# Moving the arena of a fused two-block kernel by 192 bytes: base addresses at multiples of 128 bytes

## The chip, the core and the metric

The kernel runs on one core of a Trainium2 chip. Its engines are TensorE (matmuls, weight loads), VectorE, ScalarE and GpSimd; SyncE issues most of the DMA transfers. They share SBUF, a memory of 128 partitions, and meet through semaphores. The metric is the device time of one execution in microseconds; lower is better.

## The reference

Two transformer-like blocks run one after the other on 256 tokens of 1024 features, all in float32. Cut to what matters here:

```python
def reference(x, ...):
    h = concat(meta_tokens, x)                 # 16 + 256 tokens
    h = h + token_mixer(h)                     # retention + mLSTM heads, w_in, w_out
    h = h + expert_choice_ffn(h)               # 16 experts, 34 tokens each, D_FF = 2816
    x = rmsnorm(h)[:, 16:]
    for layer in range(2):                     # second block
        x = x + rmsnorm(mixer[layer](rmsnorm(x)))           # attention / conv, then RG-LRU
        x = x + rmsnorm(memory_cross_attention(rmsnorm(x), rmsnorm(mem)))
        x = x + rmsnorm(swiglu(rmsnorm(x)))                 # D_FF = 2816
    return x

def expert_choice_ffn(h):
    ...                                        # per expert: its 34 top tokens
    hid = silu(xs @ w_gate[e]) * (xs @ w_up[e])
    y = hid @ w_down[e] * g[e]
```

The experts' weights (16 times three matrices of 1024 x 2816) are by far most of what has to be read from memory.

## The kernel before

The program is written out by hand, one instruction stream for each engine, with semaphores between them; nothing is scheduled by a tool. It has three parts, one after the other.

- Part A, the mixer of the first block, to about 200 us. Weights come in chunks of 1 MB into a ring. ScalarE writes a rounded copy of each chunk ("high") and VectorE the remainder ("low"), and TensorE makes three passes (high x high, low x high, high x low), lines 865, 883 and 1082. The moving operands are mixer_high_a, mixer_high_b and mixer_low, eight tiles of 272 columns (1088 bytes) each.
- Part B, the 16 experts, to about 1500 us. For each expert SyncE loads w_gate, w_up and w_down in quarters of 2816 KB into the ring, each as soon as TensorE has read the quarter that it replaces (line 587). `hidden` (line 1266) has the token tile xs as weights and streams the ring; the down projection (line 1349) has hidT as weights and streams the ring. In between, eight pieces of w_xkv for the second block are loaded into the arena (line 593, tile kvw) and used at line 1233.
- Part C, the second block, to the end. Chunks of 1 MB come into the ring again and are split in high (ScalarE, line 2174) and low (VectorE, line 2915). `in_part` (through `three_passes`, line 1394) has the weights chunk as stationary operand and streams input_high or input_low, 256 columns. `token_part` (line 1425) does the reverse: the stationary operand is input_high or input_low, and the ring is streamed. The output projections (`out_half`, also through line 1394) stream 512 columns of the ring.

All tiles lie in a few large SBUF tensors that are allocated one behind the other: weight_ring (W), ident, ones, hT (the residual stream), squares (SQ), rstd, vec_cols (VC), gate_w, router_w, small and arena (Z). `z(cols, at)` gives a slice of the arena, and `rounded` puts a tensor of the rounded type over a place of an existing one:

```python
def sb(name, cols, dt=F32):
    made = ctx.enter_context(nc.sbuf_tensor(name, [P, cols], dt))
    BASE[name] = nc.sbuf_base - 4 * cols
    return made
...
def rounded(name, over, at, cols):
    offset = BASE[over] + 4 * at
    return nc.alloc_sbuf_tensor_at(name, [P, cols], F32R, offset=offset)[:]
...
kvw = z(2 * 2 * D, 8192)
xs = z(KT * MPAD, 21280)
th = z(P * HF, 21808)
hidT = z(P * HF, 23216)
...
x_high = rounded("input_high", "arena", 14336, 2 * D)
x_low = rounded("input_low", "arena", 16384, 2 * D)
y_high = rounded("mixed_high", "weight_ring", CSLOTS * CSLOT, 2 * D)
```

The numbers are columns of 4 bytes. So a tile's address in a partition is the base of its tensor and four times its column. mixed_low (column 18432) and hidden_high_a (20480) lie in the arena too, mixed_high in the ring, and hidden_low_b in hT. A column number that is a multiple of 32 is an offset that is a multiple of 128 bytes.

Of the kernel before, what the change touches and what calls it, by code (L numbers as in the profile page):

```python
# [31 lines left out]
DFF = 2816  # L32
FT = DFF // P
EPS = 1e-6
ARENA = 25096
BIG = 1e30
PAD = 2

# [89 lines left out]
def build(nc, t, out):  # L128

    with ExitStack() as ctx:  # L130
        BASE = {}
# [5 lines that stand above are left out]
# [3 lines left out]
        def S(name):  # L140
            if name not in sems:
                sems[name] = ctx.enter_context(nc.semaphore(name))
            return sems[name]
# [7 lines left out]
        hT = sb("hT", KT * T)  # L151
        SQ = sb("squares", KT * T)
        RSTD = sb("rstd", T)
        VC = sb("vec_cols", 256)
        GW = sb("gate_w", KT * 16)
        RW = sb("router_w", KT * 16)
        small = sb("small", 192)
        Z = sb("arena", ARENA)

        def rounded(name, over, at, cols):  # L160
# [4 lines left out]
        def vec(name, i):  # L165
            tile, at, n = VEC_AT[name]
            return VC[:, tile * P + at + i:tile * P + at + i + 1]

        def vec_cols(name, n):
            tile, at, _ = VEC_AT[name]  # L170
            return VC[:, tile * P + at:tile * P + at + n]

        cursor = [0]

        def z(cols, at=None):
            if at is None:
                at = cursor[0]
                cursor[0] += cols
            assert at + cols <= ARENA, (at, cols)
            return Z[:, at:at + cols]  # L180
# [18 lines left out]
        lamt = small[:, 144:152]  # L199
        n4sp = small[:, 152:160]  # L200
        stat = small[:, 160:176]
        eps = small[:, 184:185]
        tiny = small[:, 185:186]


        uT = z(KT * T)
# [15 lines left out]
        rows = [z(T) for _ in range(7)]  # L222
        assert cursor[0] <= ARENA, cursor[0]
        vrow = QKP[:, 0:256]
# [41 lines left out]
        mm = z(2 * KT * 256, 12288)  # L266
        mem_gains = VC[:, 192:208]
        utok = z(TT * D, 16384)
# [2184 lines left out]
        def _(dve):  # L2453
# [41 lines left out]
            for j, n in enumerate(VEC_COUNT):  # L2495
                last = dve.tensor_copy(VC[:, P * j:P * j + n], bank[7][:, T + P * j:T + P * j + n])
            last.then_inc(S("small_ready"), 1)
# [17 lines left out]
            dve.memset(qkp[:, :, PAD + T:2 * PAD + T], 0.0).then_inc(S("small_ready"), 1)  # L2515
            dve.tensor_scalar(half_a, VC[:, B_A_AT:B_A_AT + 8], 0.5, None, ALU.mult)
            dve.tensor_scalar(half_i, VC[:, B_A_AT + 8:B_A_AT + 16], 0.5, None, ALU.mult).then_inc(S("small_ready"), 1)
            lam = VC[:, LAM_AT:LAM_AT + 8]
# [823 lines left out]
```

## Time and profile before

| | |
|---|---|
| Median of 3 runs | 2224.81 us (2224.5 to 2226.95) |
| Profiled execution, span | 2224.9 us (the page gives no other time of it) |
| TensorE busy (matmul) | 2099.5 us, 94% |
| TensorE busy (weight load) | 1310.1 us, 59% |
| VectorE busy | 780.3 us, 35% |
| ScalarE busy | 627.7 us, 28% |
| GpSimd busy | 44.6 us, 2% |
| Moved by DMA | 725.27 MB, mean 326 GB/s |

Busy times overlap, so they don't add up to the span. An engine's share of the span is an average over three parts with different limits; the chain of work that ended last tells which engine set the end in which part. Matmuls are pipelined, and the time from the start of one to the start of the next is shorter than the duration that the profile gives for one.

### The profile page before, as it was taken

The numbers are of one execution on the slowest core, as the hardware profiler recorded it, in microseconds if no ns is written. First come the engines' busy times: TensorE is split into PE (matmuls) and PEld (weight loads), VectorE is DVE, ScalarE is ACT, GpSimd is POOL, SyncE is SP. The second block draws the span as 40 slices with busy tenths as digits, with TensorE's granted clock in tenths as the row PEclk, the third lists the DMA queues.
The fourth block names the chain that finished last, engine by engine and source line by source line (L and its number), as shares of the span: only waits on it lengthen the run. The fifth ranks groups of instructions, "written<-read, shape, count | busy, mean of one in ns | idle before, by whom it ended". The sixth has DMA issues, their size and how long they took to land.

```text
span 2224.9 us, 27202 instructions
## 1 busy us (share of the span) xinstructions
PE 2099.5 (94%) x12031; PEld 1310.1 (59%) x12031; DVE 780.3 (35%) x1144; ACT 627.7 (28%) x988; POOL 44.6 (2%) x74
## 2 busy tenths in 40 slices
PE   9999999898898999989899899889999999999999
PEld 9987443333333443434333333327889998998997
DVE  8984211011010111111011011016666565876553
ACT  6564100000000000000000000005565444965442
POOL 3201000000000000000000000000000000000000
PEclk9999999999999999999999999999999999999999
DMA  7548999999999999999999999997454656554653
GB/s 235 167 136 352 417 431 428 431 428 431 428 430 430 427 429 429 428 430 429 429 430 430 429 430 430 429 425 241 146 171 155 202 184 197 174 170 151 198 189 114
DMA packets 146527, 725.27 MB, mean 326 GB/s; under 512 B 8678, under 2 KB 106522, under 8 KB 119658
## 3 DMA queue, kind: packets, MB, share of 16 engines
q1 hardware_dynamic: 145224, 721.53, 81.1%
q8 instruction: 95, 1.56, 0.3%
q0 software_dynamic: 640, 1.37, 0.2%
q10 hardware_dynamic: 546, 0.63, 0.1%
q14 instruction: 22, 0.18, 0.0%
HBM read 722.44 MB, written 1.07 MB: 325 GB/s over the span
## 4 chain that ended last, share of the span: by engine, by line
PE 65%; DMA 27%; DVE 5%; ACT 1%; issue 1%; SPq 1%; DVEq 0%; ACTq 0%
PE bank L1394 24%; PE bank L1266 18%; DMA weight_ring<-in_w_gate_dram 10%; DMA weight_ring<-in_w_up_dram 9%; DMA weight_ring<-in_w_down_dram 8%; PE bank L1349 6%; PE bank L1233 5%; PE bank L1425 3%; DVE weights_ring L2480 1%; PE bank L1197 1%; PE bank L1082 1%; DVE arena L2540 1%; PE bank L1324 1%; PE bank L1611 1%; PE bank L1741 1%
## 5 line engine op out<-in xcount | busy, mean ns | idle before, releaser
L1266 PE MATMUL bank<-weight_ring,arena 128*64 128x506 f32 x3024 | 634.6, 565 | 65.4 <-DMA weight_ring<-in_w_up_dram 42.6
L1266 PEld LDWEIGHTS bank<-weight_ring,arena 128*64 128x64 f32 x3024 | 219.8, 135 | 464.6 <-issue 374.6
L1349 PE MATMUL bank<-weight_ring,arena 128*64 128x512 f32 x1408 | 323.2, 610 | 40.1 <-DMA weight_ring<-in_w_down_dram 40.0
L2915 DVE TENSOR_TENSOR weights_ring<-weight_ring,weights_ring 128x2048 fp32r<-128x2048 f32 x110 | 249.7, 2289 | 126.3 <-ACT weights_ring L2174 125.9
L1394 PE MATMUL bank<-input_high,weights_ring 128*128 128x256 f32 x1920 | 248.3, 281 | 0.9 <-issue 0.9
L1349 PEld LDWEIGHTS bank<-weight_ring,arena 128*64 128x64 f32 x1408 | 99.2, 140 | 244.3 <-issue 185.5
L1394 PEld LDWEIGHTS bank<-input_high,weights_ring 128*128 128x128 f32 x1920 | 234.6, 188 | 2.9 <-issue 2.6
L2174 ACT ACTIVATE weights_ring<-weight_ring 128x2048 fp32r<-128x2048 f32 x109 | 205.8, 1908 | 60.2 <-DMA weight_ring<-in_w_ffn_down_dram 41.1
L2872 DVE TENSOR_TENSOR arena<-arena,bank 128x512 f32<-128x512 f32 x48 | 33.0, 688 | 498.9 <-PE bank L1233 498.9
L2070 ACT ACTIVATE arena<-bank 128x506 f32<-128x506 f32 (+1 forms) x48 | 23.5, 563 | 398.3 <-PE bank L1266 398.3
L1394 PE MATMUL bank<-input_low,weights_ring 128*128 128x256 f32 x960 | 132.3, 279 | 0.0
L1233 PE MATMUL bank<-arena 128*128 128x256 f32 x512 | 127.6, 392 | 0.0
L1233 PEld LDWEIGHTS bank<-arena 128*128 128x128 f32 x512 | 92.0, 189 | 52.7 <-issue 42.8
L1394 PEld LDWEIGHTS bank<-input_low,weights_ring 128*128 128x128 f32 x960 | 121.3, 188 | 0.0
L2090 ACT ACTIVATE squares<-bank 128x512 f32<-128x512 f32 x16 | 9.6, 597 | 382.7 <-PE bank L1349 382.7
L2040 ACT ACTIVATE squares<-bank 128x512 f32<-128x512 f32 x15 | 9.0, 597 | 367.5 <-PE bank L1197 367.5
L2861 DVE TENSOR_TENSOR hT<-hT,bank 128x512 f32<-128x512 f32 x60 | 38.6, 684 | 201.6 <-PE bank L1285 201.6
L1394 PE MATMUL bank<-weights_ring,mixed_high 128*128 128x512 f32 x320 | 93.7, 399 | 0.0
L2881 DVE SCALAR_TENSOR_TENSOR arena<-arena,bank 128x506 f32<-128x506 f32 (+1 forms) x48 | 28.0, 639 | 136.8 <-ACT arena L2070 136.8
L1394 PE MATMUL bank<-weights_ring,hidden_high_a 128*128 128x512 f32 x256 | 70.4, 395 | 0.0
L2870 DVE COPY arena<-bank 128x512 f32<-128x512 f32 x16 | 11.1, 692 | 167.5 <-PE bank L1233 167.5
L1394 PEld LDWEIGHTS bank<-weights_ring,mixed_high 128*128 128x128 f32 x320 | 59.5, 188 | 13.3 <-issue 0.2
(431 smaller groups left out, 2080.0 us busy)
## 6 DMA issues: line engine op xcount, KB each, us to landing
weight_ring<-in_w_down_dram SPq DMA_DIRECT2D x62, 2816.0 KB, 21.8
weight_ring<-in_w_up_dram SPq DMA_DIRECT2D x61, 2816.0 KB, 19.5
weight_ring<-in_w_gate_dram SPq DMA_DIRECT2D x60, 2816.0 KB, 18.9
weight_ring<-in_w_ffn_gu_dram SPq DMA_DIRECT2D x44, 1024.0 KB, 5.1
weight_ring<-in_w_ffn_down_dram SPq DMA_DIRECT2D x22, 1024.0 KB, 4.9
weight_ring<-in_w_in_dram SPq DMA_DIRECT2D x16, 1024.0 KB, 5.9
arena<-in_w_xkv_dram SPq DMA_DIRECT2D x8, 2048.0 KB, 21.2
weight_ring<-in_ab_w_in_dram SPq DMA_DIRECT2D x12, 1024.0 KB, 7.7
```

The costliest lines, as they stand in the source:

```text
L1082: last = pe.matmul(bank[pj.entries[A_OUT[n]][0]][:, 0:T], (high, low, high)[part][:, i, c], mix_low[:, T * i:T * i + T] if part == 2 else ...
L1233: last = pe.matmul(bank[7][:, 256 * a:256 * a + 256], w, x, start=(i == 0), stop=(i == 1))
L1266: last = pe.matmul(bank[first_bank + c][MPAD * half:MPAD * half + MPAD, 0:(hi - lo) * HF], xs3[:, s, :], w[:, lo:hi, HF * half:HF * half + ...
L1349: last = pe.matmul(bank[6][MPAD * half:MPAD * half + MPAD, :], hidT[:, at:at + MPAD], W[:, j * D + 512 * half:j * D + 512 * half + 512], s ...
L1394: last = pe.matmul(dst, w, y, start=start and n == 0, stop=stop and n == len(todo) - 1, skip_group_check=check)
L1425: last = pe.matmul(dst[:, 256 * t:256 * t + 256], x[:, i, tok], w[:, i, :], start=(n == 0 and i == 0), stop=(n == 2 and i == KT - 1))
L2070: act.activation(th[:, HF * lo:HF * hi], bank[c][:, 0:HF * (hi - lo)], ACT.Tanh, scale=0.5)\
L2174: act.activation(high_slot(k), raw_slot(k), ACT.Copy).then_inc(S("weights_high"), 1)
L2861: dve.tensor_tensor(rows, rows, bank[6 + n % 2][:], ALU.add).then_inc(S("scatter_taken"), 1)
L2872: ins = dve.tensor_tensor(dst, dst, bank[7][:], ALU.add)
L2881: dve.scalar_tensor_tensor(out=v, in0=v, scalar=1.0, in1=bank[c][:, 0:HF * (hi - lo)], op0=ALU.add, op1=ALU.mult)\
L2915: dve.tensor_tensor(low_slot(k), raw_slot(k), high_slot(k), ALU.subtract).then_inc(S("weights_low"), 1)
```

## The change

Four tensors of small tables lose unused columns and a spacer of 8 columns (32 bytes) is put ahead of the arena. vec_cols goes from 256 to 208 columns, small from 192 to 184 with its last two columns in use moved to 176 and 177, and the arena loses 8 unused columns at its end. Nothing else is edited: every instruction is the same, on the same engine, with the same waits and in the same order.

```diff
-ARENA = 25096
+ARENA = 25088
...
         hT = sb("hT", KT * T)
         SQ = sb("squares", KT * T)
         RSTD = sb("rstd", T)
-        VC = sb("vec_cols", 256)
+        VC = sb("vec_cols", 208)
         GW = sb("gate_w", KT * 16)
         RW = sb("router_w", KT * 16)
-        small = sb("small", 192)
+        small = sb("small", 184)
+        sb("arena_offset", 8)
         Z = sb("arena", ARENA)
...
-        eps = small[:, 184:185]
-        tiny = small[:, 185:186]
+        eps = small[:, 176:177]
+        tiny = small[:, 177:178]
```

Where the tensors begin in a partition, from the memory maps of the two built programs:

| Tensor | before, byte | past a multiple of 128 | after, byte | past a multiple of 128 |
|---|---|---|---|---|
| weight_ring | 16512 | 0 | 16512 | 0 |
| hT | 107648 | 0 | 107648 | 0 |
| squares | 116352 | 0 | 116352 | 0 |
| vec_cols | 126144 | 64 | 126144 | 64 |
| gate_w | 127168 | 64 | 126976 | 0 |
| router_w | 127680 | 64 | 127488 | 0 |
| small | 128192 | 64 | 128000 | 0 |
| arena | 128960 | 64 | 128768 | 0 |

## Rows read from the trace of the kernel before

**Rows 1.** The page: DMA rate in 40 slices; chain that ended last.

```profile
DMA  7548999999999999999999999997454656554653
GB/s 235 167 136 352 417 431 428 431 428 431 428 430 430 427 429 429 428 430 429 429 430 430 429 430 430 429 425 241 146 171 155 202 184 197 174 170 151 198 189 114
...
PE 65%; DMA 27%; DVE 5%; ACT 1%; issue 1%; SPq 1%; DVEq 0%; ACTq 0%
```

**Rows 2.** DMA: queue (packets, MB) and issues (count, KB each, us to landing).

```profile
q1 hardware_dynamic: 145224, 721.53, 81.1%
...
arena<-in_w_xkv_dram SPq DMA_DIRECT2D x8, 2048.0 KB, 21.2
...
arena<-in_w_up_dram SPq DMA_DIRECT2D x4, 1408.0 KB, 8.5
```

**Rows 3.** Line 593's loads of w_xkv; then two stretches, DMA share and GB/s last.

```profile
L593 SPq DMA_DIRECT2D arena<-in_w_xkv_dram x8: 328/432/434, 245.9 to 1214.9; - x8
...
DMA to landing us min/median/max: 12.4/21.2/24.0
...
250.00:1250.00 1000.00, 922.19 (x4404) 372.38 (x4401) 126.88 (x235) 89.60 (x148) 0.00 (x0) 0.98 1.00 429
1250.00:1450.00 200.00, 178.80 (x846) 68.52 (x846) 19.56 (x36) 16.60 (x26) 0.00 (x0) 0.98 1.01 430
```

**Rows 4.** Line 1394: duration ns min/median/max, first and last start us.

```profile
L1394 PE MATMUL bank<-input_high,weights_ring x1920: 276/279/468, 1537.5 to 2156.9; 128*128 128x256 f32 x192
L1394 PE MATMUL bank<-input_low,weights_ring x960: 276/279/283, 1539.4 to 2157.8; 128*128 128x256 f32 x192
L1394 PEld LDWEIGHTS bank<-weights_ring,mixed_high x320: 186/188/192, 1605.1 to 2179.3; 128*128 128x128 f32 x160
L1394 PEld LDWEIGHTS bank<-weights_ring,hidden_high_a x256: 187/188/189, 1820.9 to 2202.1; 128*128 128x128 f32 x128
```

**Rows 5.** The chain, in part C: start us, us, what.

```profile
1530.94 4.88 PE bank L1425 x43
1644.26 2.73 PE bank L1394 x24
1703.91 3.18 PE bank L1425 x27
1711.04 170.15 PE bank L1394 x1193
1759.92 6.13 PE bank L1394 x52
```

**Rows 6.** Line 1394 in two stretches: PE and PEld busy, granted clock, DMA.

```profile
1644.00:1648.00 4.00, 2.97 (x24) 2.79 (x24) 1.00 1.02 400
1760.00:1764.00 4.00, 4.00 (x37) 4.00 (x35) 1.00 0.84 263
```

**Rows 7.** Weight loads of the experts: duration ns min/median/max.

```profile
L1266 PEld LDWEIGHTS bank<-weight_ring,arena x3024: 132/134/229, 205.8 to 1485.8; 128*64 128x64 f32 x189
L1349 PEld LDWEIGHTS bank<-weight_ring,arena x1408: 132/137/232, 251.1 to 1509.7; 128*64 128x64 f32 x176
```

**Rows 8.** The page's groups: busy us, mean ns, idle before us.

```profile
L1266 PEld LDWEIGHTS bank<-weight_ring,arena 128*64 128x64 f32 x3024 | 219.8, 135 | 464.6 <-issue 374.6
L1349 PEld LDWEIGHTS bank<-weight_ring,arena 128*64 128x64 f32 x1408 | 99.2, 140 | 244.3 <-issue 185.5
```

**Rows 9.** VectorE lines 3217, 2861 and 2872: duration ns min/median/max.

```profile
L3217 DVE TENSOR_TENSOR mixed_high<-squares,hidden_high_a x8: 684/685/687, 1718.0 to 2086.6; 128x512 fp32r<-128x512 f32 x8
L3217 DVE TENSOR_TENSOR mixed_low<-squares,hidden_high_a x8: 684/685/686, 1761.0 to 2131.9; 128x512 fp32r<-128x512 f32 x8
L3217 DVE TENSOR_TENSOR hidden_low_b<-squares,hidden_high_b x6: 684/685/687, 1806.3 to 2165.8; 128x512 fp32r<-128x512 f32 x6
L2861 DVE TENSOR_TENSOR hT<-hT,bank x60: 680/684/689, 301.0 to 1479.3; 128x512 f32<-128x512 f32 x60
L2872 DVE TENSOR_TENSOR arena<-arena,bank x48: 687/689/689, 437.4 to 1377.9; 128x512 f32<-128x512 f32 x48
```

**Rows 10.** ScalarE lines 2296 and 2144: duration ns min/median/max.

```profile
L2296 ACT ACTIVATE mixed_high<-bank x8: 597/598/600, 1658.6 to 2016.7; 128x512 fp32r<-128x512 f32 x8
L2144 ACT ACTIVATE input_high<-bank x24: 593/597/601, 1519.4 to 2038.0; 128x512 fp32r<-128x512 f32 x24
```

**Rows 11.** The chain, in part A: start us, us, what.

```profile
107.08 3.01 PE bank L883 x24
171.91 12.31 PE bank L1082 x94
```

## The prediction, made before the changed kernel was timed

> **What bounds the kernel now.** I read the page first. Its slices show two regimes: from about 200 us to 1450 us the DMA engines are full at 417 to 431 GB/s, and outside that stretch they are not, while TensorE is busy nearly throughout [rows 1]. The chain of work that ended last says the same in shares: TensorE 65% of the span, DMA 27%, VectorE 5%, ScalarE 1% [rows 1]. So a change of addresses has four ways to act: it can change how fast DMA packets are written, how fast TensorE streams or loads operands, and how long a VectorE or a ScalarE instruction takes. It adds, removes and reorders nothing: instructions, waits and queue order of the two built programs are equal on all five engines.
>
> **What moves, and what does not.** From the memory map of the two programs: weight_ring starts at byte 16512, hT (the stream) at 107648, squares at 116352, before and after alike. All three are multiples of 128 already (129, 841 and 909 times 128) and do not move. gate_w, router_w, small and the arena move down by 192 bytes. The arena goes from 128960 (64 past a multiple of 128, 192 past one of 256) to 128768 (a multiple of both). A tile in the arena is helped only if its own offset is a multiple of 128: input_high, input_low, mixed_low, hidden_high_a, the expert input xs and the loads of w_xkv go from 64 past to aligned. The expert tiles th (offset 87232, 681.5 times 128) and hidT (92864, 725.5 times 128) go the other way, from aligned to 64 past. So half of the claim is no change at all, and the trace of before already holds the same instructions on tiles of both kinds. I price each engine from such pairs.
>
> **DMA.** Queue q1 moves 721.53 MB [rows 2]. All weight slots are in the ring and keep their addresses. Into the arena go the 8 loads of w_xkv (2048 KB each) and 4 of w_up (1408 KB) as the large ones [rows 2]. The first is issued at 245.9 us and the last at 1214.9 us, landing 12 to 24 us later [rows 3]. The stretch 250 to 1250 us, which holds nearly all of that traffic, moves 429 GB/s; the stretch 1250 to 1450 us, which has only ring loads, 430 GB/s [rows 3]. If the whole difference of 1 GB/s were the fault of unaligned writes, and all of it lay on the path, its removal would give 1000 us times 1/430, which is 2.3 us. I take 0, because 1 GB/s is the last digit of the view; the bounds are -2.3 us and 0, since no large load becomes less aligned.
>
> Here a rule speaks for the change. The Trainium skill, DMA: Bandwidth & Descriptors, section How a descriptor splits into AXI transactions, says that a descriptor which does not start at a multiple of 256 bytes first transfers from the 256-byte boundary below, and that the unused bytes cost beats of 32 bytes. For a row of w_xkv (16 KB at 192 past the boundary) that would be 6 beats on top of 512; by that rule, and as an estimate, 16 MB in such rows would take 1.2% longer than need be, some 0.5 us of the 39 us that 16.8 MB take at 430 GB/s; the sum would then be -0.5 us instead of 0. The trace neither confirms nor excludes so little, and the ring, which starts 128 past a multiple of 256, would keep its own cost under this rule.
>
> **TensorE, moving operand.** This is the term that could matter, for in the last third TensorE is the chain with few breaks: one piece from 1711 us on holds 1193 matmuls of line 1394 in 170.15 us [rows 5]. The projections (in_part, line 1394) stream input_high and input_low, 256 columns, from the unaligned arena: 1920 + 960 matmuls [rows 4]. The token parts (line 1425) stream 256 columns from the aligned ring. In the chain, 24 of the first kind take 2.73 us, 113.8 ns each, and 43 of the second take 4.88 us, 113.5 ns each [rows 5]. Elsewhere both are slower by the same: 52 of the first in 6.13 us are 117.9 ns each, and 27 of the second in 3.18 us are 117.8 ns [rows 5]. So there are two paces of streaming, at a granted clock of 1.00, the full 2.4 GHz level, in both cases [rows 6], and each pace is reached by aligned and unaligned operands alike. Alignment to 128 is worth at most 0.3 ns per matmul: 2880 times 0.3 ns is 0.9 us. I take 0, with bounds of 0.9 us either way.
>
> **TensorE, weight loads.** LDWEIGHTS of 128 columns has a median of 188 ns from mixed_high (aligned, in the ring) and 188 ns from hidden_high_a (unaligned, in the arena) [rows 4]. In the experts xs (unaligned) has a median of 134 ns and hidT (aligned) 137 ns [rows 7]. These two swap kinds; if 3 ns were due to that, xs would lose or gain 3024 times 3 ns, 9.1 us, and hidT 1408 times 3 ns, 4.2 us, with opposite signs, 4.9 us net. It is hidden: the weight-load side of TensorE sits idle 464.6 us before line 1266 and 244.3 us before line 1349 [rows 8]. Only if that cover were gone would 4.9 us show, so the term is 0.
>
> **VectorE and ScalarE.** The same subtraction of 512 columns (line 3217) into mixed_high (aligned), mixed_low (unaligned) and hidden_low_b (aligned) has medians of 685, 685 and 685 ns [rows 9]. An addition onto hT (aligned, line 2861) takes a median of 684 ns, one onto the arena (line 2872) 689 ns [rows 9]. ScalarE's copy from PSUM takes 598 ns into mixed_high and 597 ns into input_high [rows 10]. The widest gap is 5 ns in 684, 0.7%. VectorE holds 5% of the chain, 111 us, so even if every one of these instructions changed by that much it would be 0.8 us; ScalarE's 1% gives less than 0.1 us. I take 0, with bounds of 0.8 us either way.
>
> **Sum.** 0 us, with bounds of -2.3 - 0.9 - 0.8 = -4.0 us and +0.9 + 0.8 = +1.7 us. The page gives the profiled execution a span of 2224.9 us and no other time; the median of the three runs is 2224.81 us, 0.1 us below it, so the sum carries over as it stands: 2224.8 us. The runs themselves spread from 2224.5 to 2226.95 us, and I call 0.2%, 4.4 us, what a measurement of this kernel can tell from no change.
>
> **Rivals.** (1) Faster: the slower pace of 117.9 ns is a clash between operands that lie half a 128-byte line apart, and goes when ring and arena lie in step. Then 2880 matmuls fall by 4.1 ns, 11.8 us: 2213 us. It becomes visible from 1.5 ns each. For it: most of the projections run at the slower pace. Against it: the row of 24 at 113.8 ns is the same line on the same unaligned tile [rows 5], so address alone does not set the pace. Chance 0.09.
>
> (2) Slower: ring and arena in step make TensorE's two reads (weights from the ring, moving operand from the arena) meet. The nearest row for an uneven pace is line 1082, whose operands of 272 columns begin at alternating multiples of 64: 94 take 12.31 us, 131.0 ns each, against 24 in 3.01 us, 125.4 ns, at line 883 [rows 11]. That is 4.5%; on 117.9 ns it is 5.3 ns, times 2880 is 15 us: 2240 us. It too decides from 1.5 ns each. Against it: the token parts have no pace of their own, and line 883 has the same alternation as line 1082. Chance 0.05.
>
> (3) The change does nothing that the chip sees, for 64 past a line is as good as the line itself. This is the forecast: 2224.8 us, chance 0.86, its own range 2221 to 2229 us.
>
> **How the numbers follow.** Faster by over 0.2%: rival 1, 0.09. Slower: rival 2, 0.05. Within 0.2%: 0.86. For the range I take the bounds of the sum, 2220.8 and 2226.5 us, and add the spread of the runs at the upper end (2.1 us): 2228.6. Rounded outwards a little it is 2220.3 to 2229.2 us, and leaves out about the two rivals.
>
> **What the profile after would show.** Right: 429 GB/s in the stretch 250 to 1250 us, 188 ns for the weight loads, 685 ns for line 3217, the chain's projections again at 113.8 and 117.9 ns, and the same shares. Wrong would be a new pace of line 1394 (below 116 or above 119.5 ns in the long stretch from 1711 us), 431 GB/s or more where w_xkv is loaded, or an L1349 weight load above 140 ns, which would mean that hidT pays for its new place. The prediction fails if a relation between two operands' addresses counts, since the rows of before show each kind of tile but only one distance between ring and arena.

## The result, and the profile after

The changed kernel took 2228.78 us (median of 20 runs, 2227.77 to 2230.22), the kernel before in the same session 2225.32 us: a ratio of 1.0016 with an interval of 1.001 to 1.0022. That is 3.5 us more. It lies inside the predicted range (2220.3 to 2229.2 us) and inside 0.2%, but the interval does not hold 1: the change made the kernel a little slower, where the forecast was no effect at all. One execution of the kernel before took 4057.97 us and is left out.

First the page of the changed kernel, against [rows 1, 2, 8]; its span is 2227.1 us.

```profile
PE 65%; DMA 27%; DVE 5%; ACT 1%; issue 1%; SPq 0%; DVEq 0%; ACTq 0%
...
L1350 PEld LDWEIGHTS bank<-weight_ring,arena 128*64 128x64 f32 x1408 | 102.0, 143 | 252.1 <-issue 194.1
...
arena<-in_w_xkv_dram SPq DMA_DIRECT2D x8, 2048.0 KB, 21.5
```

The shares of the chain are those of before, within a point. Line numbers are one higher (line 1394 is now 1395, line 1425 is 1426). Now the stretches, as in [rows 3]: us, then busy PE, PEld, DVE, ACT and POOL, granted clock, DMA share and GB/s.

```profile
250.00:1250.00 1000.00, 928.74 (x4392) 371.80 (x4388) 125.33 (x231) 88.64 (x145) 0.00 (x0) 0.98 1.00 429
1250.00:1450.00 200.00, 180.88 (x854) 69.32 (x856) 19.55 (x36) 16.59 (x26) 0.00 (x0) 0.98 1.00 430
1712.00:1874.00 162.00, 162.00 (x1149) 151.89 (x1148) 86.25 (x62) 69.95 (x55) 0.00 (x0) 1.00 0.57 189
```

DMA runs as before, 429 and 430 GB/s. So does the clock: it is granted in full, 1.00, in part C.

The chain in part C shows the difference: start us, us, what. A piece of the chain is a stream of matmuls with nothing between them, so its time over its count is the pace from one start to the next.

```profile
1527.93 5.98 PE bank L1426 x48
1643.08 2.85 PE bank L1395 x24
1693.66 5.70 PE bank L1426 x48
1710.30 171.11 PE bank L1395 x1193
2049.24 172.53 PE bank L1395 x1199
```

And the same pieces before, apart from those in [rows 5]:

```profile
1530.07 5.76 PE bank L1425 x48
1660.76 2.83 PE bank L1394 x24
1694.47 5.44 PE bank L1425 x48
2047.95 171.56 PE bank L1394 x1199
```

The reader is to see two things. First, the pace. Leaving aside the pieces of 2.9 us and more, which both kernels have, 24 matmuls of the projections take one time after the change, 2.85 us (2.84 to 2.88), which is 2.85 / 24 = 118.8 ns each. Before there were two, 2.83 / 24 = 117.9 ns and 2.73 / 24 = 113.8 ns [rows 5]. Second, the length of part C. The first piece of part C and the end of its last give the sum: before 2047.95 + 171.56 - 1530.07 = 689.44 us, after 2049.24 + 172.53 - 1527.93 = 693.84 us, 4.4 us more. Summed over this chain, the 3732 matmuls of line 1394 take 538.14 us before and 542.09 us after, 3.95 us more, and the 480 of line 1425 take 58.07 and 58.83 us, 0.76 us more; the rest takes 0.3 us less. The two longest pieces alone carry 1.9 us (0.96 + 0.97). Part C began 2.1 us earlier in this execution than in the one before. The kernels below, profiled once each, reach the same piece between 1527.13 and 1528.84 us, whatever their addresses, so I don't put those 2.1 us down to the change.

### The profile page after: what moved, and what is told of

Its sections match the earlier page's. It is cut to its first block, busy times and chain, and to the rows that moved or that the text cites. A ratio compares the mean times of both kernels' runs of the same rounds, so it can differ in the third digit from the quotient of the medians.

```text
span 2227.1 us, 27202 instructions
## 1 busy us (share of the span) xinstructions
PE 2110.9 (95%) x12031; PEld 1314.9 (59%) x12031; DVE 779.8 (35%) x1144; ACT 627.1 (28%) x988; POOL 44.1 (2%) x74
## 4 chain that ended last, share of the span: by engine, by line
PE 65%; DMA 27%; DVE 5%; ACT 1%; issue 1%; SPq 0%; DVEq 0%; ACTq 0%
PE bank L1395 24%; PE bank L1267 17%; DMA weight_ring<-in_w_up_dram 12%; DMA weight_ring<-in_w_down_dram 9%; PE bank L1350 7%; DMA weight_ring<-in_w_gate_dram 6%; PE bank L1234 5%; PE bank L1426 3%; DVE weights_ring L2481 1%; PE bank L1198 1%; DVE arena L2541 1%; PE bank L1083 1%; PE bank L1325 1%; PE bank L1612 1%; PE bank L1635 1%
## 5 line engine op out<-in xcount | busy, mean ns | idle before, releaser
L1350 PE MATMUL bank<-weight_ring,arena 128*64 128x512 f32 x1408 | 333.6, 626 | 40.2 <-DMA weight_ring<-in_w_down_dram 40.2
L1350 PEld LDWEIGHTS bank<-weight_ring,arena 128*64 128x64 f32 x1408 | 102.0, 143 | 252.1 <-issue 194.1
## 6 DMA issues: line engine op xcount, KB each, us to landing
arena<-in_w_xkv_dram SPq DMA_DIRECT2D x8, 2048.0 KB, 21.5
```

Of the source, the lines that this page charges most:

```text
L1350: last = pe.matmul(bank[6][MPAD * half:MPAD * half + MPAD, :], hidT[:, at:at + MPAD], W[:, j * D + 512 * half:j * D + 512 * half + 512], s ...
```

## The experiments

Two theories stood against each other at first. Theory 1: what counts is how far TensorE's moving tile lies from its stationary tile (arena against ring), whatever the alignment of either. As it was first recorded it took this distance modulo 128: slow at a multiple of 128, as before halfway between. The rival: alignment itself counts (the arena at a multiple of 128), or the moved tables do. "Distance" below means the address of the arena tile less that of the ring tile, modulo 256, since the runs came to need 256 and not 128. It is (128960 - 16512) mod 256 = 64 before and 128 after; the tiles' own columns add multiples of 256.

**Tables alone.** vec_cols and small are trimmed as in the change (gate_w and router_w lose nothing, they only move), and a wider spacer puts the arena back at 128960: distance 64.

```diff
-        sb("arena_offset", 8)
+        sb("arena_offset", 56)
```

> The small tables are trimmed and moved as in the change, the arena stays at byte 128960 as before. After the change the second block (from the first matmul of line 1234/1350 that no longer waits for an expert's weights, about 1475 us, to the end) is 4.3 us longer than before, and the projections of 256 columns follow each other at 118.8 ns instead of 117.9. Theory 1 (the distance between ring and arena, now a multiple of 128, disturbs TensorE's two reads): 1.0000 of before, pace 117.9. Theory 2 (the arena's own alignment does it): the same here, 1.0000. Theory 3 (the tables' places, or chance): 1.0016, pace 118.8.

**Arena at 128896**, a multiple of 128 as in the change, but at distance 0.

```diff
-        sb("arena_offset", 8)
+        sb("arena_offset", 40)
```

> As the change, but the arena 128 bytes further up, at 128896: a multiple of 128 still, and now in step with the ring modulo 256 too. Theory 1 (distance to the ring is a multiple of 128): slow, 1.0016, pace 118.8 ns. Theory 2 (arena aligned to 128): slow, 1.0016. A variant of either with 256 in place of 128 would make this one differ: further from before (over 1.002) if ring and arena in step modulo 256 is what hurts, 1.0000 if the arena at a multiple of 256 is.

**Ring up by 64.** The arena stays at 128768 as in the change, the ring goes to 16576: arena aligned, distance 64 again.

```diff
+        sb("ring_offset", 16)
...
-        small = sb("small", 184)
-        sb("arena_offset", 8)
+        small = sb("small", 176)
```

> Ring, ident, ones, stream, squares and tables 64 bytes further up, the arena at 128768 as in the change: arena aligned, ring 64 past a multiple of 128, the distance 64 past one as before. Theory 1 (distance): 1.0000, pace 117.9. Theory 2 (the arena's own alignment): 1.0016, pace 118.8.

**Both 64 past a multiple of 128.** The ring at 16576 and the arena at 128832: nothing aligned, distance 128.

```diff
+        sb("ring_offset", 16)
...
-        small = sb("small", 184)
-        sb("arena_offset", 8)
+        small = sb("small", 176)
+        sb("arena_offset", 16)
```

> Ring 64 bytes up and the arena 64 bytes up too: both 64 past a multiple of 128, the distance a multiple of 128. Theory 1 (distance): slow, 1.0016, pace 118.8. Theory 2 (the arena's own alignment): 1.0000, pace 117.9.

In the last two, the two columns in use at the end of small move to 60 and 61. The four were measured against the same runs of the kernel before (2224.24 us, 2216.28 to 2227.07):

| Kernel | Arena | Distance | Median us (lowest to highest) | Ratio to before |
|---|---|---|---|---|
| tables alone | 64 past | 64 | 2224.87 (2219.8 to 2226.77) | 1.0005 (0.9995 to 1.0015) |
| arena at 128896 | aligned | 0 | 2228.35 (2227.19 to 2230.25) | 1.0025 (1.0015 to 1.0035) |
| ring up by 64 | aligned | 64 | 2224.29 (2219.89 to 2226.37) | 1.0 (0.999 to 1.0011) |
| both 64 past | 64 past | 128 | 2229.81 (2229.49 to 2230.18) | 1.0032 (1.0021 to 1.0043) |

The split goes by the distance and not by alignment: two kernels at distance 64, one with its arena aligned and one not, run as before; the two at 0 and at 128, one with ring and arena aligned and one with neither, are slower. The tables have no effect that these runs can tell (1.0005, at most 1.0015), and part C with them is as long as before, 689.56 us against 689.44. The chain of each shows the pace, first tables alone:

```profile
1658.13 2.73 PE bank L1395 x24
1651.40 2.83 PE bank L1395 x24
1708.30 170.16 PE bank L1395 x1193
```

Arena at 128896:

```profile
1660.81 2.87 PE bank L1395 x24
1711.01 170.70 PE bank L1395 x1193
```

Ring up by 64:

```profile
1659.90 2.73 PE bank L1395 x24
1710.07 165.97 PE bank L1395 x1193
```

Both 64 past:

```profile
1660.78 2.85 PE bank L1396 x24
1711.20 171.12 PE bank L1396 x1193
```

At 64 there are 2.73 and 2.83 us, at 128 2.85, at 0 2.87. The piece of 1193 at distance 0 is shorter than at 128 although its projections are slower (2.87 / 24 = 119.6 ns); the sweep below explains a part of that. And the piece of 1193 took 170.16 us in one kernel at distance 64 and 165.97 us in another: the same stream, both at the same distance, 4.2 us apart. Theory 1 had no word for two paces at one distance.

**Distance 192.** The changed kernel with the tiles of part C moved up by 64 bytes in the arena. (mixed_high in the ring, hidden_low_b in hT and hidden_high_b at the arena's start stay.)

```diff
-        x_high = rounded("input_high", "arena", 14336, 2 * D)
-        x_low = rounded("input_low", "arena", 16384, 2 * D)
-        y_low = rounded("mixed_low", "arena", 18432, 2 * D)
+        x_high = rounded("input_high", "arena", 14352, 2 * D)
+        x_low = rounded("input_low", "arena", 16400, 2 * D)
+        y_low = rounded("mixed_low", "arena", 18448, 2 * D)
...
-        WORK = 20480
+        WORK = 20496
```

> The changed kernel with its aligned arena, but the operand tiles of the second block (input_high, input_low, mixed_low and everything from WORK on) 16 columns, 64 bytes, further up inside it. Theory 1 (what counts is the distance of each of these tiles from the weights in the ring, modulo 128): the loss goes, 1.0000 of before, pace 117.9 ns or the lower 113.3. Rival (the loss sits in the arena's base, that is in the experts or the first mixer too): 1.0016 as after the change.

**The same edit on the kernel before**, whose distance goes from 64 to 128 by it.

> The kernel before, with the same operand tiles of the second block 64 bytes further up, nothing else moved: they come to lie a multiple of 128 from the ring (a multiple of 128, odd, as after the change). Theory 1: slow, 1.0016 to 1.003, pace 118.8 ns to 120 and no stretch at 113.3. Rival (the arena's base as a whole): 1.0000.

Both stand against the same runs of the kernel before (2225.21 us). The changed kernel with the shift took 2213.8 us (2213.47 to 2215.79), a ratio of 0.995 (0.9937 to 0.9964); the kernel before with the same shift 2229.7 us (2228.6 to 2231.36), 1.0022 (1.0013 to 1.0031). One edit of four numbers has opposite signs on two bases, and the second is the slowdown of the change brought about with every tensor at its old base. The first is a miss for Theory 1 as recorded: modulo 128 the distances 64 and 192 are one, and it expected 1.0000. Distance 192:

```profile
1527.39 5.94 PE bank L1426 x48
1658.10 2.73 PE bank L1395 x24
1708.14 165.45 PE bank L1395 x1193
2040.05 166.87 PE bank L1395 x1199
```

Before with the shift, distance 128:

```profile
1660.58 2.85 PE bank L1394 x24
1711.11 171.08 PE bank L1394 x1193
```

At 192 the long pieces are 5.7 us shorter each than after the change, and part C as a whole takes 2040.05 + 166.87 - 1527.39 = 679.53 us, 9.9 us less than before and 14.3 us less than after.

**Distances by themselves.** A kernel of matmuls alone; the reference's computation is left out. For each distance it streams 96 matmuls in the form of the projections (line 112 has distance 0, and each second line 16 bytes more, to line 142), then some in the form of the token parts (lines 144 to 150: 0, 64, 128, 192) and 48 of 512 columns (lines 152 to 158: the same four). The whole is done once with the other engines still and once with them at work (lines 162 to 208).

```diff
+            for n in range(16): pe.matmul(bank[6][:, 0:P], ident[:], ident[:], start=True, stop=True)
+            for n in range(96): pe.matmul(*in_args(n, 64), **ends(n, 24))
```

> Not the reference's computation: it leaves out all of it and only streams matmuls, 96 for each distance between the tile of the weights and the moving tile (0 to 240 bytes in steps of 16 modulo 256), as the projections do, then the two reverse forms at 0, 64, 128 and 192; all once with the other engines quiet and once with VectorE, ScalarE and DMA at work. Theory 1: at distances 0 and 128 the matmuls of 256 columns follow each other at 118.8 to 120 ns, at 64 and 192 at 113.3 or 117.9; with the engines quiet as well, since only TensorE's own two reads meet. Rival (the other engines' accesses to SBUF are what meets TensorE's): 113.3 at every distance while they are quiet.

Its chain, the whole of a line in each row:

```profile
28.32 11.51 PE bank L112 x96
...
88.08 11.31 PE bank L120 x96
...
117.89 11.52 PE bank L124 x96
...
132.98 10.93 PE bank L126 x96
...
147.48 11.40 PE bank L128 x96
...
207.27 11.31 PE bank L136 x96
...
326.72 10.92 PE bank L152 x48
...
341.22 11.19 PE bank L154 x48
...
355.98 11.15 PE bank L156 x48
...
370.70 10.99 PE bank L158 x48
...
492.84 10.93 PE bank L176 x96
```

Divided by 96: distance 0 is 119.9 ns, 64 is 117.8, 96 is 120.0, 112 is 113.9, 128 is 118.8, 192 is 117.8. All sixteen lie between 113.9 and 120.0 ns. With 512 columns the order is another one: 227.5 ns at 0, 233.1 at 64, 232.3 at 128, 229.0 at 192. So at distance 0 the 256-column matmuls lose and the 512-column ones gain. The piece of 1193 is a mix: 935 of 256 columns, and 258 of 512, of which 204 have their stationary tile in the arena. From 128 to 0 the first lose 1.0 us by these paces and the 204 gain 1.0. By that it should be about as long at 0 as at 128; that it was 0.4 us shorter stays unexplained. The second pass repeats the first (10.93 us again at 112), with VectorE and ScalarE busy and DMA moving data, as the stretches show (same columns as above):

```profile
100.00:380.00 280.00, 280.00 (x2229) 272.13 (x2228) 0.00 (x0) 0.00 (x0) 0.00 (x0) 1.00 0.00 1
450.00:740.00 290.00, 290.00 (x2313) 282.10 (x2312) 150.74 (x66) 144.04 (x76) 0.00 (x0) 1.00 0.33 131
```

So the disturbance needs nobody but TensorE itself. It isn't simply a matter of lying in step, for 96, which is out of step, is as slow as 0. What this kernel did not show is the fast pace at 64 and 192, which the full kernels have.

**Distance 112**, the best one of the sweep of the projections' form, in the full kernel: the changed kernel with the tiles of part C up by 240 bytes (UP is 60 columns). Since the tensors are placed 16 bytes lower, each tile is a slice that leaves out its first 4 columns.

```diff
-        x_high = rounded("input_high", "arena", 14336, 2 * D)
+        x_high = rounded("input_high", "arena", 14336 + 56, 2 * D + 4)[:, 4:]
...
-        WORK = 20480
+        WORK = 20480 + UP
```

> The changed kernel with the operand tiles of the second block 60 columns, 240 bytes, further up in the arena: 112 past a multiple of 256 from the ring, the one distance at which the sweep held 113.3 ns steadily. If the sweep's pace carries over: part C loses 5.5 ns on most of 2880 matmuls of line 1395 against the change, some 15 us, so about 2213 us, 0.995 of before, unless the token parts and the 512-column matmuls, not swept at this distance, give it back. Rival (the sweep's value is an accident of how its stream begins): anywhere between 0.995 and 1.003.

**Distance 192 on the kernel before**: its tiles up by 128 bytes, no table trimmed, the arena 64 past as it was.

```diff
-        x_high = rounded("input_high", "arena", 14336, 2 * D)
+        x_high = rounded("input_high", "arena", 14368, 2 * D)
...
-        WORK = 20480
+        WORK = 20512
```

> The kernel before with nothing moved but the operand tiles of the second block, 128 bytes up: 192 past a multiple of 256 from the ring instead of 64. By the distance modulo 256: the same as the run with the changed arena and tiles up by 64, 0.995 of before, about 2213 us. Rival (that run was fast for its aligned arena base, not for its distance): 1.0000.

Against the same runs of before (2221.35 us, 2217.65 to 2227.67), distance 112 took 2215.82 us (2215.39 to 2216.04), 0.997 (0.9959 to 0.9981), and distance 192 2215.33 us (2214.83 to 2215.88), 0.9969 (0.9958 to 0.9981). Both gained less than expected (about 2213 us, 0.995 of before). For the second, part of this is the yardstick: the kernel before had a median of 2225.21 us in the session of the first run at 192 and 2221.35 here, on another chip. The two kernels at 192 themselves lie within 1.6 us, and their parts C within 0.2 us, though the arena and the tables have other bases. Distance 112:

```profile
1651.42 2.76 PE bank L1396 x24
1708.42 166.09 PE bank L1396 x1193
```

Distance 192 on the kernel before:

```profile
1528.84 5.94 PE bank L1425 x48
1652.88 2.75 PE bank L1394 x24
1709.67 165.36 PE bank L1394 x1193
2041.42 166.78 PE bank L1394 x1199
```

At 112 the projections run at 2.76 / 24 = 115.0 ns, not at the sweep's 113.9. With all kernels profiled, part C from the first of these pieces to the end of the last goes by the distance:

| Distance | Part C, us |
|---|---|
| 0 | 693.05 (arena at 128896) |
| 64 | 689.44 (before), 689.56 (tables alone), 685.69 (ring up by 64) |
| 112 | 680.72 |
| 128 | 693.84 (after), 693.83 (both 64 past), 694.17 (before with the shift) |
| 192 | 679.53 (changed base), 679.36 (base of before) |

For 64 and 128 this holds with the ring at either of two places. For 0, 112 and 192 the ring never moved, and the two kernels at 192 have tiles whose addresses differ by 256, so that there a part of the moving tile's own address is not told apart from the distance.

The paces of the small kernels also give the size. From 128 to the fast pace of 192 (113.4 ns, next experiment), 935 matmuls of 256 columns gain 5.4 ns each and 160 of the wide ones 3.3 ns (the 44 of hidden_high_b did not move): 5.6 us for the piece of 1193, against 5.66 us measured. So nearly all of the long piece runs at the fast pace at 192, though 5 of the shorter pieces of 24 still take 2.83 us on the changed base.

**Two paces.** Matmuls alone again; the reference's computation is left out. It sweeps the token form over all sixteen distances (lines 113 to 143) and then streams 48 matmuls of the projections' form, with one odd matmul of 4, 20, 36 and so on to 116 columns ahead of them, so that the stream begins at another time within its period: eight starts at distance 64 (lines 178 to 199) and at 192 (202 to 223), four each at 128, 112 and 0.

```diff
+            pe.matmul(bank[5][:, 0:20], ident[:], ident[:, 0:20], start=True, stop=True)
+            for n in range(48): pe.matmul(*in_args(n, 64), **ends(n, 24))  # 20
```

> Not the reference's computation, all of it left out: streams of matmuls only. The reverse forms (weights from the arena, 256 or 512 moving columns from the ring) at all 16 distances, then the projections' form at 64, 192, 128, 112 and 0 with one odd matmul of 4 to 116 columns ahead, which shifts the phase in which the stream begins. Theory 1 with two stable paces: at 64 and 192 some phases give 113.3 ns and others 117.8, at 128 always 118.8, at 0 always 120. Rival (pace is set by the distance alone): every phase the same.

Its chain; the rows x2 hold the odd matmul:

```profile
88.62 10.89 PE bank L121 x96
...
133.00 11.52 PE bank L127 x96
...
502.92 0.12 PE bank L177 x2
503.04 5.76 PE bank L178 x48
...
512.37 0.13 PE bank L180 x2
512.50 5.54 PE bank L181 x48
...
586.64 5.75 PE bank L205 x48
...
596.10 5.53 PE bank L208 x48
...
651.81 5.78 PE bank L226 x48
```

At distance 64 the stream after 4 columns takes 5.76 us and that after 20 columns 5.54 us, on the same addresses; with the odd matmul 5.88 and 5.67 us, 4.4 ns for each of the 48. One start of eight fell on the slow side at distance 64, three of eight at 192, and none changed anything at 128, 112 or 0. Line 121 is the token form at distance 64: 10.89 / 96 = 113.4 ns here, while the same form at the same distance took 11.31 us in the first sweep. So at 64 and at 192 there are two paces, and where in the period the stream begins chooses between them. (For 192 the fast pace is 5.53 + 0.15 us, the slow one 5.75 + 0.13 us, the second number being the odd matmul's.) Two of them in one kernel is what [rows 5] had shown and what I had read as two paces of everything.

The token form has its own order: line 127 is distance 112, the best for the projections, and takes 11.52 / 96 = 120.0 ns there. In the full kernel at 112 the 480 matmuls of the token parts take 59.45 us, against 58.57 us at 192 on the kernel before, which is a part of what that kernel failed to gain.

## Why the prediction was wrong

- **TensorE, moving operand** is the step that failed. It said: "each pace is reached by aligned and unaligned operands alike. Alignment to 128 is worth at most 0.3 ns per matmul". The first sentence holds and the experiments bear it out. But the term priced alignment of one operand, when the change also changed a relation between two: in before the projections and the token parts have only one distance, 64. The term was 0 with bounds of 0.9 us either way; part C took 4.4 us more in the profiled pair, and the whole kernel 3.5 us more by the medians. By the paces at which before ran mostly, 117.9 against 118.8 ns, 2880 matmuls of the projections are 2.6 us, where line 1394 as a whole took 3.95 us more; the stretches at 113.8 ns, which distance 128 doesn't have, are a part of the rest. The token parts add 0.76 us. The sign of being wrong was also set too wide: 118.8 ns is inside its 116 to 119.5.
- **Rival 2** had the sign, and a relation between the two operands as its mechanism. That they meet because they lie in step is not shown: 96, out of step, is as slow as 0, and what inside TensorE meets is open. Its price of 5.3 ns per matmul came from line 1082, whose tiles of 272 columns lie 1088 bytes apart and so step through four distances, 64 bytes at a time; 0.9 to 5 ns was measured, most of it at the low end. "It too decides from 1.5 ns each" was too coarse: 1 ns is visible when the runs lie close together. Its "against" failed as well: at 0, 64, 128 and 192 the token form is as fast or slow as the projections' in the sweep, having the same two tiles the other way round.
- **Rival 1** took 117.9 ns for a clash of operands that lie half a line apart and 113.8 ns for its absence. Both are paces of one distance. That 113.8 ns is within reach for nearly all of part C was right, and distance 192 collects it; going into step was the wrong way.
- **DMA**: 0 us was right. 429 and 430 GB/s again, and the loads of w_xkv land in 21.5 us where they took 21.2 [rows 2]. The other kernels have 21.1 to 21.9 us, with the arena at multiples of 256 and off them alike. The Trainium skill, DMA: Bandwidth & Descriptors, How a descriptor splits into AXI transactions, tells its rule of bytes that are fetched ahead of a descriptor's start. The change moved the place that is written and left the rows that are read where they were, so the prediction's -0.5 us stretched the rule; no run here shows such a gain.
- **Weight loads**: right, and the price of 3 ns was for nothing. The medians of the experts' loads are 134 and 137 ns as before [rows 7]. The profile's mean for hidT is 143 ns against 140 [rows 8], above the 140 that the prediction had named as a sign; but it is 144 ns with hidT at its old place (tables alone) and 138 ns with it at its new one (distance 192), so it doesn't follow the address. The idle time before them is still 252.1 us.
- **VectorE and ScalarE**: right. After the change line 3217's subtraction into mixed_low, which went from 64 past to aligned, has a median of 686 ns, where it was 685 [rows 9] (ns min/median/max):

```profile
L3218 DVE TENSOR_TENSOR mixed_low<-squares,hidden_high_a x8: 681/686/689, 1760.6 to 2133.7; 128x512 fp32r<-128x512 f32 x8
```

- **The starting point**: the prediction set the span of the profiled execution, 2224.9 us, beside the median time. In the runs that give both, the time is 1.8 or 1.9 us longer than the span (2228.94 and 2227.1 us after the change), so the profiled execution of before took some 2226.7 us (an estimate), more than its median. The forecast went by the median and didn't suffer.
- The last sentence of the prediction named the hole ("if a relation between two operands' addresses counts"), yet it got 0.05. A hole that no row covers should have had the chance that an unknown has, not that of its nearest rival.

What stays open: what in TensorE makes the distance count, why two distances have two paces, and why part C of the kernel before ran mostly at the slower of its two when seven starts of eight gave the faster in the small kernel. Part A was not taken apart; its piece of 94 took 12.31 us before [rows 11] and 12.29 us after.

## What to carry to other kernels

When a change moves buffers, write down not only each address but the differences between the operands that one instruction reads together; if before has only one value of it, its effect is unknown and not zero. Where TensorE is the chain, try the distance between stationary and moving tile in a small kernel of matmuls, since a shift of 64 to 128 bytes decides here over 0.5% of the whole: 2213.8 us at 192 against 2229.7 at 128 in one session. Sweep each form that the kernel uses, since 112 was the best distance for one and among the worst for another. A sweep of one start is not enough, as the start can choose between two paces.

## What the hardware showed that I had not expected

- Back-to-back pairs of a weight load and a matmul of 128 x 128 by 256 columns (rounded fp32) run at 113.4 to 120 ns over 96 of them, at the full granted clock, by the distance of the two operands modulo 256 bytes. The Trainium skill, TensorE: Matmul & The Clock Gate, Step-by-step: what each phase is for, gives the streamed and the loaded operand a read port each, independent of one another. The runs differ from what one would take from that: with all other engines still, 96 matmuls take 10.93 us at one distance and 11.51 us at another. The same page, Back-to-back issue gap, has N / 2.4 + 2.5 ns for an isolated matmul, an estimate of 109.2 ns for 256 columns, and says that in a stream of loads and matmuls both set the spacing. No stream here reached 109.2 ns.
- The spread of a whole kernel's runs can come from the addresses. At distance 64 the kernel before reaches from 2216.28 to 2227.07 us, at 128 (the kernel before with the shift) the runs reach from 2228.6 to 2231.36, at 112 from 2215.39 to 2216.04 us; at 192, which has two paces too, they lie within 2.3 us. The 32 runs of before in the first of these sessions fall into three groups: 2 up to 2216.83 us, 12 from 2220.01 to 2222.3 and 18 from 2224.15 on, some 4 us from each to the next, as between the pieces of 165.97 and 170.16 us. That the two paces at 64 make this spread is argued from this, and not shown run by run. It also means that the cost of the change depends on the group: in the session of the result all 19 runs of before lay from 2224.19 us on, so 3.5 us is the cost against its slowest group.
